# Leaving out TensorE's products on constants during the routing of a one-core decoder layer

## What is computed

```python
z = jax.nn.gelu(h @ w_in)                 # 2048 -> 4096
u, v = jnp.split(z, 2, axis=-1)
v = rmsnorm(v, v_gain)
sv = einsum('hts,bcshd->bcthd', w_s * causal, v5) + b_s
return (u * sv) @ w_out                   # 2048 -> 2048
```

```python
probs = softmax(xf @ router_w)
sel = (probs + router_b).reshape(n, 4, 4)
grp = argmax(sum of the two largest of each group)
idx = the two largest of that group; gw = probs[idx] / their sum
for each block of tokens of an expert e:
    hid = silu(xb @ w_gate[e]) * (xb @ w_up[e])
    yb  = hid @ w_down[e]                 # weighted by gw, added to its tokens
```

## Time and profile before

| | us |
|---|---|
| three runs | 1214.67, 1215.97, 1218.34 |
| median of the runs | 1215.97 |
| the profiled execution, its own time | 1215.37 |
| span of that execution in the trace | 1213.2 |

### The profile page before, as it was taken

The page is one execution under the profiler, slowest core; times in us unless marked ns, Lnnn a source line. Parts: engine busy times, 40 slices in busy tenths (PEclk is TensorE's granted clock), DMA queues, the critical chain, the costliest instruction groups (busy, mean ns, idle before and its releaser), DMA issues.

```text
span 1213.2 us, 12020 instructions
## 1 busy us (share of the span) xinstructions
PE 1145.6 (94%) x5201; PEld 523.5 (43%) x5201; DVE 371.7 (31%) x562; ACT 110.3 (9%) x187; POOL 7.5 (1%) x24
## 2 busy tenths in 40 slices
PE   8999999999999999999989898989999898989996
PEld 7888877887333333333323232323232333222321
DVE  6867787776212111112211111111111111111112
ACT  1303002012010000000000000000000000000003
POOL 0200000000000000000000000000000000000000
PEclk9999999999999999999999999999999999999999
DMA  9856554597999999999999999999999999999996
GB/s 358 328 198 188 198 173 143 200 419 315 390 428 420 431 433 429 432 430 431 429 432 429 432 432 431 432 432 432 432 432 431 429 431 431 431 432 430 426 418 245
DMA packets 36303, 460.70 MB, mean 380 GB/s; under 512 B 4360, under 2 KB 5920, under 8 KB 21664
## 3 DMA queue, kind: packets, MB, share of 16 engines
q1 hardware_dynamic: 36208, 459.97, 91.1%
q10 hardware_dynamic: 48, 0.01, 0.0%
HBM read 457.87 MB, written 2.10 MB: 379 GB/s over the span
## 4 chain that ended last, share of the span: by engine, by line
PE 63%; DMA 34%; DVE 1%; ACT 1%; issue 0%; SPq 0%; ACTq 0%; DVEq 0%
PE bank L1258 24%; DMA blocks<-in_moe_w_gate 10%; DMA late<-in_moe_w_gate 9%; DMA late<-in_moe_w_up 8%; PE bank L1327 8%; PE kept L1052 4%; PE kept L1050 4%; PE kept L1051 4%; DMA blocks<-in_moe_w_down 4%; PE bank L1050 4%; PE bank L1052 3%; PE bank L1051 3%; DMA blocks<-in_moe_w_up 3%; PE kept L1230 3%; PE kept L1212 2%; PE kept L1221 1%
## 5 line engine op out<-in xcount | busy, mean ns | idle before, releaser
L942 DVE TENSOR_TENSOR acc<-acc,kept 128x512 f32<-128x512 f32 x120 | 77.1, 683 | 452.1 <-PE kept L1230 452.1
L1258 PE MATMUL bank<-blocks,xg_a 128*64 128x512 f32 x832 | 193.9, 609 | 20.7 <-DMA blocks<-in_moe_w_gate 19.1
L1327 PE MATMUL bank<-blocks,sil 128*64 128x512 f32 x800 | 176.4, 595 | 11.0 <-DMA blocks<-in_moe_w_down 11.0
L1258 PE MATMUL bank<-blocks,xg_b 128*64 128x512 f32 x752 | 166.6, 595 | 4.7 <-DMA blocks<-in_moe_w_gate 2.7
L1258 PEld LDWEIGHTS bank<-blocks,xg_a 128*64 128x64 f32 x832 | 59.3, 139 | 149.4 <-issue 142.4
L699 DVE TENSOR_TENSOR w_lo<-blocks,w_hi 128x1024 fp32r<-128x1024 f32 x96 | 117.7, 1226 | 3.2
L1327 PEld LDWEIGHTS bank<-blocks,sil 128*64 128x64 f32 x800 | 55.7, 137 | 122.3 <-issue 102.8
L1258 PEld LDWEIGHTS bank<-blocks,xg_b 128*64 128x64 f32 x752 | 52.3, 137 | 115.8 <-issue 100.0
L969 DVE TENSOR_TENSOR sil<-sil,bank 128x512 f32<-128x512 f32 x16 | 11.0, 687 | 248.0 <-PE bank L1258 248.0
L692 DVE CAST w_hi<-blocks 128x1024 fp32r<-128x1024 f32 x96 | 67.0, 698 | 65.0 <-PE kept L1052 30.4
L1230 PE MATMUL kept<-y,back 64*128 64x512 f32 x240 | 67.7, 641 | 0.0
(11 more groups left out here) (211 smaller groups left out, 943.6 us busy)
## 6 DMA issues: line engine op xcount, KB each, us to landing
blocks<-in_moe_w_down SPq DMA_DIRECT2D x21, 4096.0 KB, 40.2
blocks<-in_moe_w_gate SPq DMA_DIRECT2D x20, 4096.0 KB, 39.4
blocks<-in_moe_w_up SPq DMA_DIRECT2D x20, 4096.0 KB, 40.3
blocks<-in_a_w_in SPq DMA_DIRECT2D x31, 1024.0 KB, 5.5
late<-in_moe_w_gate SPq DMA_DIRECT2D x6, 4096.0 KB, 33.3
late<-in_moe_w_up SPq DMA_DIRECT2D x6, 4096.0 KB, 40.0
blocks<-in_moe_w_down SPq DMA_DIRECT2D x11, 2048.0 KB, 12.0
blocks<-in_moe_w_gate SPq DMA_DIRECT2D x9, 2048.0 KB, 11.8
```

The lines of the kernel that those rows point to most:

```text
L942: V.tensor_tensor(acc[:, b, cols], acc[:, b, cols], bank[5 + j % 3][:, :], ALU.add)\
L1258: ins = T.matmul(bank[unit // 2 % 2][c * TOK:(c + 1) * TOK, :], xg(unit // 4 * 8 + unit % 2 * 4 + s), weights[:, s * F + c * BANK:s * F + ...
L1327: ins = T.matmul(bank[2 + c // 2][at:at + TOK, :], hidden, weights[:, s * D + c * BANK:s * D + (c + 1) * BANK], start=(j == 0 and s == 0), ...
```

## The change

Two of the four calls of `keep_warm` go: the 20 products between the logits and the ranks, and the 4 products between the ranks and the gather. Nothing else is changed, and no wait is added or removed. What the two calls wrote was read by nothing.

```diff
             last.then_inc(logits_done, 1)
-            keep_warm(4, 20)
-
             pe.wait_ge(assigned_ready, 1)
...
                          start=True, stop=False)
-
-            keep_warm(4, 4)
 
             pe.wait_ge(pick_ready, 1)
```

## The result

| | before | changed |
|---|---|---|
| median of 20 runs each | 1215.99 us | 1218.67 us |
| lowest and highest | 1214.67 to 1218.34 | 1217.11 to 1221.97 |
| the profiled execution, its own time | 1215.37 | 1218.57 |
| span | 1213.2 | 1216.4 |
| mean granted TensorE clock | 0.993 | 0.984 |

The ratio is 1.0022, with a 95% interval of 1.0016 to 1.0028: a loss of 0.22%, clear of noise and under the 0.3% named in the prediction. There are 48 fewer matmul records, and the kernel is slower.

What follows compares the result with a forecast made beforehand. It took the weight stream as the bound, with one hole ahead of the first item. Small products 0.1 plus gather 1.6 gave 1.7 us, so 1215.97 + 1.7 = 1217.7 us, range 1215.2 to 1220.6 us.

Steps and rivals of the forecast that it cites:

- The bound: Weight stream full to 1187 us except one hole before L409's issue at 304.97 us; delay there counts in full.
- rival A: In the routing, the clock holds or the thin stream absorbs the loss: 1216.0 us, chance 0.17.
- The products cost nothing on the path: Before ranks and gather, removing the products gives back 0 to 0.1 us at each place; taken as 0.
- Rival C: In the routing, the products have an unseen cost and their absence speeds it up: 1215.8 us, chance 0.04.
- The fall: PE, idle 4.63 us between logits and ranks, loses its clock between about 295 and 297.5 us.
- The length of the low spell: From the fall to about the gather's end; PE works 2.8 to 3.4 us before full clock is back.
- The sum: Ahead of L409's issue: small products 0.1 us plus gather 1.4 to 1.7, taken as 1.6; 1.7 us in all.
- the term of the first item: At the first item's start: nothing in the forecast, since the clock would be back; 1.7 us in the upper end.
- rival B: Gather, transposes and first item's first unit at half clock: 5.2 us, 1221.2 us; chance 0.13, or 0.06 with 3 to 3.6 us.
- a clock of 0.50 in the first item: Sign in the first item that the prediction is wrong and the routing stays slow to its end.
- The transposes: Between gather and first item: no loss in the forecast, about 1.3 us long; 1.29 us doubled in the upper end.
- The median: Whole kernel: 1217.7 us, from the 1215.97 us median of three runs plus 1.7; a loss of 1 to 3 us, chance 0.6.

Runs made afterwards that it cites:

- the 24 products: Kernel before the change with 24 more products on constants ahead of the gather, behind the wait for pick: 1221.20 against 1216.80 us, ratio 1.0041.
- ten early: Kernel before the change with 10 products instead of 20 between logits and ranks, and none before the gather: 1218.84 against 1216.80 us, ratio 1.0019.

## Why the prediction came out right, and where its steps did not

**The bound.** Right: in both traces of the changed kernel the last load follows L409 after the time of the kernel before, to 0.1 us, and a delay of PE counts ahead of the first item and not in item 3. One reading was off: I called 193 GB/s the thinnest pair of microseconds, and the earlier trace rows has one of 188, which changes nothing in rival A. Rival A, that part of the loss is absorbed, is out by the trace of the 24 products (5.49 us at the issue, 5.66 at the end).

**The products cost nothing on the path.** Right: the ranks start 5.26 us after the fold without them, 5.25 with them. Rival C, that they slow the routing in a way not seen, is out.

**The fall.** Right that it comes, in both traces of the changed kernel. Wrong in its time: I had it at 295 to 297.5 us, from waits that were 2.2 to 4.2 us old when the clock fell; it fell 1.0 and 1.5 us after the last product in the two traces of the changed kernel (294.1 and 294.8 us), and 4.0 us after it in the one without the 20 products (297.3 us). In the rows I used PE had run dense products up to the wait, here it had run a few short ones with a pause among them. That can't be the whole reason, since the kernel without the 20 products had run the same and lost its clock 2.5 to 3 us later; what sets the moment is open.

**The length of the low spell.** This is the step that failed. I let it end with the gather, since in four falls PE had worked 2.8 to 3.4 us when the clock came back. Here it lasted 13.7 us and PE worked 3.69 us on the gather, 1.34 us on the transposes and 2.9 us in the first item before it ended. The sum was 0.1 + 1.6 us; the trace has 0.02 + 1.74 - 0.09 + 1.42. The gather was sized nearly rightly, 1.74 against 1.4 to 1.7; the term of the first item, 1.42 us, was put at nothing and was missing, and the result of that execution, 3.2 us, lies between my forecast of 1.7 and rival B. What I called the mechanism of B, the first dense products at half clock, did occur, in both traces. I had named a clock of 0.50 in the first item as a sign that the prediction is wrong, and by that sign this step is wrong. B's price of 5.2 us was too high in the transposes, next, and a little in the first item, 1.42 us against 1.7.

**The transposes.** I doubled them for B's upper end, 1.3 us more. They took 1.34 instead of 1.29 us with the clock at 0.50 from 303 to 305 us. The first of the four small products took 0.21 instead of 0.19 us. The Trainium skill, "TensorE: Matmul & The Clock Gate", section "Single matmul latency", gives formulas for a single bfloat16 product by which a short one hardly depends on the clock; by them eight of 64 columns would lose 8 x 0.04 = 0.3 us, an estimate. The trace agrees that they hardly slow: the eight float32 records lost 0.05 us together.

**The median.** The forecast was 1217.7 and the median is 1218.67 us, inside the range. That it lies so near is in part luck: with the sum of the trace, 3.2 us, in place of 1.7 the same reckoning gives 1219.2 us, also inside the range, but with a loss above the 1 to 3 us of the forecast. The profiled execution of the kernel before had no fall in the routing, but kernels with all 24 products do lose the clock at the first item in some executions: the two traces with 12 more products show it, at 303.4 and 306.8 us, and the first of them is the kernel before up to its fourth item. So the kernel before probably pays for a fall now and then too. That would fit the medians, which differ by 2.7 us and not by the 3.2 us of the two profiled executions, but it isn't shown: how often it falls in the kernel before was not counted.

## What to carry to other kernels

Before counting PE's filler as waste, look at what comes after it: here the full stream of weights forgave PE 2.8 us in item 3 and nine falls of the clock, and forgave nothing just ahead of the place where the stream waited for PE. There, compare the times from the issue that ends the hole to the end of the kernel; if they are the same in all versions, only the part ahead of that issue is worth working on. And filler may have to cover the idle stretch whole: here half of it, or four products after the clock had fallen, gave the median of none at all. Nothing between ten and twenty products was tried.

## What the runs showed of the hardware that I had not expected

- The granted clock fell 1.0, 1.5 and 4.0 us after PE's last product (changed kernel twice, and without the 20 products), in the gather 1.7 us behind an idle stretch of 2.31 us (ten early), and in two of the kernels with all products 0.8 and 0.9 us into the first item, behind pauses of 0.66 and 0.3 us around short transposes, while several idle waits of 2.7 us behind dense products left it at 1.00.
- It stayed low for 13.7 us in the changed kernel, though PE had been busy for 3.69 of the 4.3 us from 298.9 us on, and came back 2.9 us into the first item's dense products.
- At half clock the gather of 512 columns took 3.69 instead of 1.94 us, the products of 128 columns 2.05 instead of 1.14 us, the transposes of 64 columns 1.34 instead of 1.29 us. Of the products here only those of 128 and 512 columns paid for the low clock.
